# A fused transformer kernel: memory values inside the causal attention, and an own buffer for the last expert's down weights

## What is computed

```python
h = rms_norm(x, ln1_w);  proj = h @ w_in
y_rnn = recurrent_group(...)                       # 512 wide
y_att = chunk_band_attention(q, k, v, rel_bias)    # 8 heads of 64
mixed = concat([rms_norm(y_rnn, gn_rnn_w), rms_norm(y_att, gn_att_w)])
x = x + mixed @ w_out
x = x + memory_cross_attention(rms_norm(x, ln2_w), mem_n, xq_w, xk_w, xv_w, xo_w)
x = x + hierarchical_moe(rms_norm(x, ln3_w), ...)  # 32 experts, 1024 -> 512 -> 1024, top 2
```

## Time and profile before

| | |
|---|---|
| Time, median of 3 runs | 2410.89 us (2410.87 to 2411.92) |
| Profiled execution | time 2413.93 us, span 2411.8 us |
| PE busy | 2195.8 us, 91% of the span |
| DVE, ACT, POOL busy | 66%, 49%, 9% |
| Chain that ended last | PE 76%, DVE 11%, ACT 8%, issue 4%, DMA 1% |
| Mean granted PE clock | 0.957 |

### The profile page before, as it was taken

One profiled execution on the slowest core, in us unless ns is written; L12 is line 12 of the kernel. 1 busy time (PEld: TensorE's weight loads), 2 busy tenths in 40 slices (PEclk: granted clock), 3 DMA queues, 4 the chain that ended last, 5 costly groups with the idle time before them and its releaser, 6 DMA issues.

```text
span 2411.8 us, 27159 instructions
## 1 busy us (share of the span) xinstructions
PE 2195.8 (91%) x10362; PEld 1741.0 (72%) x10362; DVE 1584.2 (66%) x1884; ACT 1187.5 (49%) x1437; POOL 205.1 (9%) x155
## 2 busy tenths in 40 slices
PE   6998898889999999993988989999989798999997
PEld 4786577677777787772855778888766466888885
DVE  6447543468888888885677476465568767655565
ACT  4535533357777777775466342222245554322223
POOL 1000000021111111110010011020100100211020
PEclk9998899989999999996999999999999999999998
DMA  5242031469999999975210113223222002232321
GB/s 193 91 151 97 18 123 35 179 162 362 357 359 350 356 363 357 351 290 213 73 52 17 53 70 105 88 88 107 103 87 70 36 1 76 100 105 83 109 88 53
DMA packets 48814, 359.98 MB, mean 149 GB/s; under 512 B 12224, under 2 KB 13416, under 8 KB 21456
## 3 DMA queue, kind: packets, MB, share of 16 engines
q1 hardware_dynamic: 36880, 340.89, 38.5%
q0 software_dynamic: 10752, 13.60, 1.7%
q10 hardware_dynamic: 1088, 4.19, 0.4%
HBM read 360.71 MB, written 25.72 MB: 160 GB/s over the span
## 4 chain that ended last, share of the span: by engine, by line
PE 76%; DVE 11%; ACT 8%; issue 4%; DMA 1%; ACTq 0%; SPq 0%; DVEq 0%; POOLq 0%
PE bank L1031 40%; PE bank L498 14%; PE bank L1942 10%; DVE split_products L562 3%; ACT split_products L726 2%; PE bank L1967 2%; PE bank L1744 1%; PE bank L488 1%; PE bank L1729 1%; ACT S L1808 1%; PE bank L1758 1%; DVE X L1282 1%; DVE split_weights L1237 1%; ACT S L1819 1%; ACT S L761 1%
## 5 line engine op out<-in xcount | busy, mean ns | idle before, releaser
L1031 PE MATMUL bank<-split_x_high,split_weights 128*128 128x512 f32 x2144 | 672.5, 394 | 31.2 <-DVE split_x_low L1251 14.7
L1245 ACT ACTIVATE split_weights<-ring 128x2048 fp32r<-128x2048 f32 (+1 forms) x122 | 228.2, 1872 | 648.2 <-PE bank L1031 526.5
L1031 PEld LDWEIGHTS bank<-split_x_high,split_weights 128*128 128x128 f32 x2144 | 407.8, 190 | 122.2 <-issue 36.8
L1237 DVE TENSOR_TENSOR split_weights<-ring,split_weights 128x2048 fp32r<-128x2048 f32 (+1 forms) x122 | 276.6, 2268 | 228.5 <-ACT split_weights L1245 228.4
L1031 PE MATMUL bank<-split_products,split_weights 128*128 128x512 f32 x1200 | 334.4, 395 | 4.5 <-DVE split_products L1437 4.5
L1031 PE MATMUL bank<-split_x_low,split_weights 128*128 128x512 f32 x800 | 312.5, 391 | 0.0
L1031 PEld LDWEIGHTS bank<-split_products,split_weights 128*128 128x128 f32 x1200 | 229.0, 191 | 53.9 <-DVE split_products L1437 6.0
L498 PE MATMUL bank<-split_products 128*128 128x512 f32 x768 | 189.7, 396 | 11.8 <-DVE split_products L562 11.8
L498 PE MATMUL bank<-split_x_low,split_products 128*128 128x512 f32 x768 | 192.4, 400 | 6.8 <-DVE split_x_low L562 4.7
L498 PE MATMUL bank<-split_x_high,split_products 128*128 128x512 f32 x768 | 190.0, 397 | 8.0 <-DVE split_x_high L562 8.0
L562 DVE TENSOR_TENSOR split_products<-ring,split_products 128x2048 fp32r<-128x2048 f32 x63 | 144.4, 2293 | 57.9 <-ACT split_products L726 52.8
(11 more groups left out here) (421 smaller groups left out, 2973.4 us busy)
## 6 DMA issues: line engine op xcount, KB each, us to landing
ring<-in_expert_down_w SPq DMA_DIRECT2D x32, 2048.0 KB
ring<-in_expert_gate_w SPq DMA_DIRECT2D x31, 2048.0 KB, 8.3
ring<-in_expert_up_w SPq DMA_DIRECT2D x31, 2048.0 KB, 7.8
ring<-in_ffn_w_up SPq DMA_DIRECT2D x44, 1024.0 KB, 4.8
ring<-in_w_in SPq DMA_DIRECT2D x26, 1024.0 KB, 4.9
ring<-in_ffn_w_down SPq DMA_DIRECT2D x16, 1024.0 KB, 4.7
ring<-in_w_out SPq DMA_DIRECT2D x12, 1024.0 KB, 4.8
ring<-in_ffn_w_down SPq DMA_DIRECT2D x8, 768.0 KB, 4.1
```

What stands on the lines that cost most here:

```text
L1031: mm = pe.matmul(acc[:, :], w[:, u, k, m], x, start=first and q == 0, stop=last and q == 2)
L1237: st.tell(dve.tensor_tensor(w[:, 1, 0:ks, 0:nc_], raw_half(g)[:, :, 0:nc_], as_f32(w[:, 0, 0:ks, 0:nc_]), ALU.subtract), wl_done)
L1245: st.tell(act.activation(WHL[g % 2][:, 0, 0:ks, 0:nc_], raw_half(g)[:, :, 0:nc_], ACT.Copy), wh_done)
```

## The change

1. In the causal attention the scores use banks 0 and 1 alone (`depth=1`; the layers' attention keeps 2), and PE waits for the add of the pair just before. In every odd step p up to 15, between the values of pair p - 2 and the turning of pair p - 1, `memory_values` makes one tile of memory values (24 matmuls) in bank 2 or 3. ACT copies the tile out in `inside(p)`, and after every second one converts the next weight unit (16 to 19); DVE makes the low parts of units 16 to 18 behind pairs 4, 8 and 12, and of 19 behind the last.
2. The statistic and root of the recurrent norm stand behind the second of the four key units. The split of the normed recurrent half leaves the attention: ACT makes its four high parts between the last square and the root of the attention norm, DVE its four low parts behind unit 19's.
3. The last expert's down weights have an own buffer, `QKVG[:, 8:16]`, which is free by then. SP issues their load without a wait, right behind the loop; their first half is split inside the last block, the second behind it.

```diff
-            for u in range(4):
-                token_unit(14 + u, A_XV + 2 * u, 2, *mem_in)
-            pe.wait_ge(tile_free, A_XQ)
-            pe_pairs(pe, att_cfg[0], 0)
+                if u == 1:
+                    rms("gn_rnn", ((a_add, 8, SUM),))
+            pe.wait_ge(tile_free, A_XV)
+            def memory_values(p):
+                if p % 2 and p < 2 * DC:
+                    n = p // 2
+                    g = 14 + n // 2
+                    pe.wait_ge(wl_done, g + 1)
+                    if n >= 2:
+                        pe.wait_ge(tile_free, A_XV + n - 1)
...
+            pe_pairs(pe, att_cfg[0], 0, fill=memory_values)
+            pe.wait_ge(tile_free, A_XQ)
...
-                        if p >= 2:
-                            pe.wait_ge(s["shifted"], before + 2 * (p - 2) + i + 1)
+                        if p >= cfg["depth"]:
+                            pe.wait_ge(s["shifted"], before + 2 * (p - cfg["depth"]) + i + 1)
...
@@ dve inside(p) @@
-                if 4 <= p < 8:
-                    c = p - 4
-                    dve.wait_ge(a_hi, DC + c + 1)
-                    st.tell(dve.tensor_tensor(MIXL[c], G[:, c, :], as_f32(MIX[:, c, :]), ALU.subtract), a_lo)
+                if p in (4, 8, 12):
+                    unit_low(dve, st, 15 + p // 4)
...
@@ act inside(p) @@
-                if 3 <= p < 7:
-                    high(DC + p - 2, MIX[:, p - 3, :], G[:, p - 3, :])
+                if p % 2:
+                    m = p // 2
+                    evac(VM[:, m % 2, (m // 2) * 256:(m // 2 + 1) * 256], half, b=2 + m % 2)
+                    if m % 2:
+                        unit_high(act, st, 16 + m // 2)
...
             st.tell(act.activation(square[1], S[:, 15, :], ACT.Square), a_sq)
+            for c in range(HC):
+                high(DC + c + 1, MIX[:, c, :], G[:, c, :])
             root(2, HC)
...
@@ moe_sync @@
-            down(final, e)
+            sp.dma_start(LAST_DOWN, expert_w(A["expert_down_w"], e)).then_inc(last_landed, 16)
+        LAST_DOWN = QKVG[:, 8:16, :].rearrange("p a n -> p (a n)")
...
@@ act block_of_experts @@
+                if last:
+                    weights_high(4, 16, b * 6 + 5, "last")
                 act.wait_ge(a_turned, b + 1)
...
-            weights_high(4, nb * 16, nb * 6)
-            weights_high(5, nb * 16, nb * 6)
+            weights_high(5, 16, nb * 6, "last")
...
@@ dve block_of_experts @@
+                if last:
+                    weights_low(4, b * 6 + 7, "last")
                 dve.wait_ge(a_high, b + 1)
...
-            weights_low(4, nb * 6 + 1)
-            weights_low(5, nb * 6 + 2)
+            weights_low(5, nb * 6 + 2, "last")
```

More of the change, by code:

```diff
@@ L220, in build @@
                     values=[(r, lambda kt, h=h: V[:, kt, h * 64:(h + 1) * 64]) for h, r, tt in halves(j, t)]))
-        att_cfg.append(dict(pairs=pairs, sems=att, dest=lambda c: S[:, 12 + c, :]))
+        att_cfg.append(dict(pairs=pairs, depth=1, sems=att, dest=lambda c: S[:, 12 + c, :]))
         units = []
@@ L960, in build @@
         att_chunk = (6, 7, 2, 3)
-        l_cfg = dict(pairs=l_pairs, sems=latt, dest=lambda c: XH[:, att_chunk[c], :], low=True)
+        l_cfg = dict(pairs=l_pairs, depth=2, sems=latt, dest=lambda c: XH[:, att_chunk[c], :], low=True)
         def layer_sync(sp):
@@ L1714, in _, with pe_pairs @@
             layer_gpsimd(pool, st)
-        def pe_pairs(pe, cfg, l, first=None):
+        def pe_pairs(pe, cfg, l, first=None, fill=None):
             s, pairs = cfg["sems"], cfg["pairs"]
@@ L1726, in pe_pairs @@
                     for i, (q, k) in enumerate(x["scores"]):
-                        if p >= 2:
-                            pe.wait_ge(s["shifted"], before + 2 * (p - 2) + i + 1)
-                        pe.matmul(bank[2 * (p % 2) + i][:, 0:x["keys"]], q, k, start=True, stop=True).then_inc(s["scored"], 1)
+                        if p >= cfg["depth"]:
+                            pe.wait_ge(s["shifted"], before + 2 * (p - cfg["depth"]) + i + 1)
+                        pe.matmul(bank[2 * (p % cfg["depth"]) + i][:, 0:x["keys"]], q, k, start=True, stop=True).then_inc(s["scored"], 1)
                 p = step - 2
@@ L1746, in pe_pairs @@
                                 mm.then_inc(s["summed"], 1)
+                if fill:
+                    fill(step)
                 p = step - 1
@@ L2013, in _ @@
                 split_unit(10 + u, **tiles(A_XK + 2 * u), count=mem_in, n=MEM)
-            rms("gn_rnn", ((a_add, 8, SUM),))
-            for u in range(4):
-                token_unit(14 + u, A_XV + 2 * u, 2, *mem_in)
+                if u == 1:
[8 more added lines that the diff above has]
+                        pe.wait_ge(tile_free, A_XV + n - 1)
+                    tok = slice((n % 2) * P, (n % 2 + 1) * P)
+                    hi, lo = mem_in
+                    for k in range(DC):
+                        for q, (u, x) in enumerate(((0, hi(k)), (0, lo(k)), (1, hi(k)))):
+                            mm = pe.matmul(bank[2 + n % 2][:, 0:256], x[:, tok], WHL[g % 2][:, u, k, :], start=(k == 0 and q == 0), stop=(k == DC - 1 and q == 2))
+                    mm.then_inc(tile_done, 1)
+            pe_pairs(pe, att_cfg[0], 0, fill=memory_values)
             pe.wait_ge(tile_free, A_XQ)
-            pe_pairs(pe, att_cfg[0], 0)
             rms("gn_att", ((a_add, 10, SUM), (a_sq, 16, square[1])))
@@ L2161, in _ @@
                 add_squares(DC, m, HC)
[L2162 to L2167, removed]
+            unit_low(dve, st, 12)
+            unit_low(dve, st, 13)
+            dve.wait_ge(a_rstd, 2)
+            for c in range(HC):
+                st.tell(dve.scalar_tensor_tensor(G[:, c, :], G[:, c, :], col("gn_rnn", c), rstd[:, :], ALU.mult, ALU.mult), a_hn)
+            unit_low(dve, st, 14)
+            unit_low(dve, st, 15)
             dve.wait_ge(s_bias, 1)
             def inside(p):
-                if 4 <= p < 8:
-                    c = p - 4
-                    dve.wait_ge(a_hi, DC + c + 1)
-                    st.tell(dve.tensor_tensor(MIXL[c], G[:, c, :], as_f32(MIX[:, c, :]), ALU.subtract), a_lo)
+                if p in (4, 8, 12):
+                    unit_low(dve, st, 15 + p // 4)
                 if p == 10:
@@ L2181, in _ @@
             dve_pairs(dve, st, att_cfg[0], 0, inside)
+            unit_low(dve, st, 19)
+            for c in range(HC):
+                dve.wait_ge(a_hi, DC + c + 1)
+                st.tell(dve.tensor_tensor(MIXL[c], G[:, c, :], as_f32(MIX[:, c, :]), ALU.subtract), a_lo)
             normed_split(2, DC + HC, HC, lambda c: S[:, 12 + c, :], lambda c: col("gn_att", c), lambda c: S[:, 12 + c, :],
@@ L2312, in _ @@
                     evac(KM[:, c, :], half)
[L2313 to L2317, removed]
-            def inside(p):
-                if 3 <= p < 7:
-                    high(DC + p - 2, MIX[:, p - 3, :], G[:, p - 3, :])
+                if u == 1:
+                    root(1, HC)
+            def inside(p):
+                if p % 2:
[3 more added lines that the diff above has]
+                        unit_high(act, st, 16 + m // 2)
                 if p in (5, 9, 13):
```

11 lines of the change are left out of this document (7 added, 4 removed).

## The result

| | before | after |
|---|---|---|
| Time, median | 2411.4 us (2410.87 to 2412.47, 4 runs) | **2391.6 us** (2389.5 to 2394.74, 4 runs) |
| Ratio to before | | 0.9918, 95% interval 0.9906 to 0.993 |
| Profiled execution: time, span | 2413.93, 2411.8 us | 2391.76, 2389.7 us |
| PE busy, mean granted clock | 2195.8 us, 0.957 | 2184.7 us, 0.967 |

The forecast was 2393.9 us, in a range of 2386 to 2405. The profiled run of after was already 1.2 us late at an instruction both kernels share ahead of the stage (VectorE's first addition of squares for the recurrent norm: 159.19 us before, 160.42 after). Times in the stage are compared from there.

What follows compares the result with a forecast made beforehand. A ring of TensorE, VectorE and ACT was taken to bound the attention, TensorE the memory values. Attention stage -9.8 (-12.5 + 2.7 tail) and buffer -7.2 gave -17.0: from 2410.89 to 2393.9 us, range 2386 to 2405.

Steps and rivals of the forecast that it cites:

- Start of the attention: With the root inside the memory keys, first scores start at 182.6 us, 23.3 us earlier than 205.94.
- Period: Four attention pairs take 17.6 us: TensorE's 8.9, two memory-value groups 5.8, waits 1.6 (512-key values) and 1.3 (256-key values).
- Score waits: Attention scores with one bank pair wait for the previous pair's add: put at 0, upper bound 11 us in all.
- if scores wait for the add: Sign in the attention that would show the forecast wrong; the other was groups at 5 us beyond the second.
- VectorE no longer bounds: In the attention, VectorE has 14.2 us of work in a period of 17.6 us, so it does not bound.
- Half clock in the first group, +2.7: The attention's first memory-value group probably runs at half clock after TensorE stands still, adding 2.7 us.
- the 5.7 taken over from the stage before: Attention stage forecast as four periods of 17.6 us plus 5.7 us outside them, 76.1 us in all.
- Tail: Between last square and fifth chunk's low part, ACT's four high parts stall TensorE: +2.2 to 2.8 us, taken 2.7.
- Buffer: At the expert stage's end, own buffer for the last down weights: -7.2 us, with 0.4 for an uncovered register load.
- The ragged clock: Rival: attention's mean clock stays near 0.75, +2.5 to +4 us a period, 10 to 16 in all; chance 0.15.
- The early transfer: Rival: the last down weights' early load delays the previous expert's by 3 to 5 us, costing +2 to +3; chance 0.08.
- 14.7 x 1.8: Rival of half clock throughout the attention: TensorE's period work becomes 26.3 us, total 2426 us; chance 0.04.

Runs made afterwards that it cites:

- halves_first: The changed kernel with half a memory-value group (12 matmuls) in every step, ahead of the attention's values: 2384.7 us, 0.9904 of before.
- depth1_only: The kernel before with one pair of score banks in the causal attention instead of two, nothing else: 2412.7 us, 0.9996 of before.
- ahead_tail: The changed kernel with whole groups ahead of the scores and two of ACT's four high-part copies before the last attention output: 2393.9 us, 0.9922 of before.
- after_again: The changed kernel run once more, unaltered, on another chip: 2391.9 us, 0.992 of before.

## Why the prediction was right, and where its terms were off

- **Start of the attention.** Forecast 182.6; 184.13, less the 1.2 of drift 182.9. Right, and the root inside the keys costs about what it said.
- **Period.** Forecast 17.6, measured 17.62. The two waits came as 1.27 (forecast 1.6) and 0.75 (1.3), with 0.21 ahead of the 384-key values that the sum did not have: 2.2 us in all for 2.9. TensorE was busy for 15.4 us and not 14.7. So 0.7 us stood in the other term; the next point says why.
- **Score waits.** The step "that add ends before TensorE arrives: I put it at 0" failed in its reason. TensorE does arrive before it: 1.93 - 1.13 = 0.80 us at each 512-key product (1.13 is what it takes in halves_first at its best). But 0.80 + 0.75 is 1.55 us, the wait that the kernel before has ahead of the same values (1.56 at 245.92); depth1_only shows the same exchange. The cost of 0 held, as a wait already in the sum. The prediction's own sign, that it is wrong "if scores wait for the add", came true while the time was right: the sign named a wait that costs nothing there.
- **"VectorE no longer bounds"** held at 17.6, but by 1.5 us only. The 14.2 us of work were 13.5 and 14.1; the 2.2 us of waits for exponentials were not counted. This is why covering TensorE's waits gave half of what I expected of it.
- **Half clock in the first group, +2.7.** The group ran at 4.42 us (forecast 5; by its own rows the slower group costs 2.3 to 2.4 us, not 2.7) and the clock was 0.69 until 191, as forecast. But from the first scores to the end of the last square it took 260.33 - 184.13 = 76.2 us, the 76.1 of the sum without this term. VectorE's 256-key additions, at 187.86, 207.26, 224.88 and 242.49 us, show a first period of 19.4 and then 17.6 twice: the slow start did cost 1.8 us. What lies outside the four periods is then 3.9 us and not the 5.7 taken over from the stage before, which ran at a clock of 0.75 and lost some of its start in that remainder. So the step that failed is "to this I add 2.7 us" on top of a remainder measured at a low clock: 2.6 us too many, most of what the stage came out better (-12.6 against -9.8). That the remainder held the clock's loss is worked out, not tried, and the first period varies with the run: 19.1 to 20.5 us in the five kernels that order this part alike.
- **Tail.** Forecast +2.2 to 2.8, taken 2.7, measured 8.15 - 6.06 = +2.1 with a stall of 1.17 us. The lower end was right; TensorE's earlier start did not add to it.
- **Buffer.** Forecast -7.2, measured 15.4 - 7.9 = -7.5. The register load, put at 0.4, costs nothing: ScalarE's copy at 1079.63 follows the one at 1079.15 directly. The Trainium skill's floor of 0.6 us for such a load ("DMA: Bandwidth & Descriptors", "Latency and other measured facts") does not show there.
- **Rivals.** The ragged clock, to which the rule of the Trainium skill on small idles between groups ("TensorE: Matmul & The Clock Gate", "A second HAM failure mode: psum-queue depth-cycling") gave its chance, did not come: gaps of 0.2 to 1.3 us in every period and a clock of 1.00 for 70 us. It came in part in ahead_tail: the clock fell to 0.50 four times, behind waits of 1.84 us (three) and 3.02 us. The early transfer took 13.7 us, against 8.4 for the median of such transfers; it went out 1.9 us behind the one ahead. The slowing that the rival feared is there: the one ahead took 10.8 us, the longest of its kind in that run. It landed at about 1066.4, some 0.2 us before ScalarE began with it, so it cost nothing, but with hardly any room left: ScalarE converts it 12.6 us ahead of the last block's second copy, in before (1078.20, 1090.78) as in after (1066.54, 1079.15). Two prices among the rivals were added up wrongly: 14.7 x 1.8 is 26.5 and not 26.3 (some 0.7 us more in that time), and 19.6 us with a wait of 1 is +3 a period and not +2.5. Neither would have moved the forecast.

The sum of -17.0 became -20.1 in the profiles and -19.8 in the medians: 2.8 us too little for the attention and 0.3 for the buffer.

## What to carry to other kernels

When work is put into an engine's gaps, add up the other engines of the ring too: VectorE's work plus its waits for ScalarE made 15.5 of a period of 16.1 us here, and covering more of TensorE's waits gained nothing beyond that. A high busy share doesn't name the bound; a piece of work that only some periods have does, by whether the period grows with it. A wait that appears where a buffer was taken away can cost nothing, as here, if the same engine waited right behind it for the same chain; compare the period, not the wait. A large early transfer is worth only part of its gain while the conversion behind it keeps its old place in the order.

## What was not expected of the hardware

- The same pause may or may not cost the clock. Between 152 and 158 us TensorE stands still for 2.7 us in all fourteen profiles, and is busy without a gap after that; the clock from 158 to 161 us is 0.50 in after_again and 1.00 in the changed kernel's first profile. Four of the fourteen profiles fell, and lost 1.5 to 2.6 us there, the largest difference between runs of the same code in this stage.
- The 2 MB of the last down weights took 13.7 us to land when issued 1.9 us behind another 2 MB, against 7.67 where they went first and others followed; the transfer ahead of them took 10.8 us.
- The granted clock stayed at 1.00 over 70 us with TensorE busy for 86% of them (60.27 of 70), where it was 0.75 at 69% in the kernel before.
